# Padding a ring of split weights by 64 bytes a slot

## The reference, cut to what matters

```python
h = rmsnorm(x); u = h @ hgrn_w_in          # 2048 -> 10240
m = gated_recurrence(u) @ hgrn_w_out       # 2048 -> 2048
x = x + rmsnorm(m)
x = x + rmsnorm(conv_ffn(rmsnorm(x)))      # 2048 -> 11264, 5632 -> 2048
proj = rmsnorm(x) @ w_in_2                 # 2048 -> 7184
x = x + concat(stick_breaking, gated_delta) @ w_out_2
x = x + cross_attention(rmsnorm(x), rmsnorm(mem))
x = x + conv_ffn_2(rmsnorm(x))
return rmsnorm(x)
```

## Time and profile before

| | us |
|---|---|
| median of 3 runs | 2696.56 |
| lowest, highest | 2696.28, 2697.19 |
| the profiled execution | 2697.01 |
| its span, first to last instruction | 2695.2 |
| TensorE matmuls busy in it | 2683.5 |
| VectorE, ScalarE busy | 1971.6, 1335.3 |

### The profile page before, as it was taken

The page is one execution under the profiler, slowest core; times in us unless marked ns, Lnnn a source line. Parts: engine busy times, 40 slices in busy tenths (PEclk is TensorE's granted clock), DMA queues, the critical chain, the costliest instruction groups (busy, mean ns, idle before and its releaser), DMA issues.

```text
span 2695.2 us, 47424 instructions
## 1 busy us (share of the span) xinstructions
PE 2683.5 (100%) x17616; PEld 2291.9 (85%) x17616; DVE 1971.6 (73%) x2721; ACT 1335.3 (50%) x1679; POOL 133.9 (5%) x138
## 2 busy tenths in 40 slices
PE   9999999999999999999999999999999999999998
PEld 8888888888888888888888888878888888888887
DVE  6888888878888888644466677767678888885444
ACT  6455555455444444433465566665644444443443
POOL 0211121210000000000000000000000000000000
PEclk9999999999999999999999999999999999999999
DMA  7555555475555555655645544355455555556554
GB/s 245 180 165 172 165 168 173 161 196 170 189 187 187 187 187 187 195 187 187 218 139 181 170 145 139 134 171 186 150 190 187 187 187 187 187 188 197 185 184 150
DMA packets 136197, 481.68 MB, mean 179 GB/s; under 512 B 14880, under 2 KB 19120, under 8 KB 135680
## 3 DMA queue, kind: packets, MB, share of 16 engines
q1 hardware_dynamic: 134160, 472.06, 53.2%
q0 software_dynamic: 1376, 7.46, 0.8%
q10 hardware_dynamic: 528, 0.26, 0.0%
HBM read 477.63 MB, written 2.10 MB: 178 GB/s over the span
## 4 chain that ended last, share of the span: by engine, by line
PE 82%; DVE 8%; issue 4%; DMA 3%; ACT 2%; DVEq 1%; SPq 0%; ACTq 0%
PE acc L442 29%; PE acc L444 15%; PE acc L465 8%; PE acc L467 8%; PE acc L466 8%; PE acc L414 4%; DMA raw<-stream 3%; DVE wts L362 3%; PE acc L415 2%; ACT wts L355 2%; DVE cy L2313 2%; DVE cin L392 1%; DVE half L380 1%; PE ps L1406 1%; PE ps L740 1%
## 5 line engine op out<-in xcount | busy, mean ns | idle before, releaser
L442 PE MATMUL acc<-hs,wts 128*128 128x512 f32 x4640 | 1626.8, 394 | 0.0
L362 DVE TENSOR_TENSOR wts<-raw,wts 128x1024 fp32r<-128x1024 f32 x888 | 1061.9, 1227 | 525.0 <-ACT wts L355 524.3
L355 ACT ACTIVATE wts<-raw 128x1024 fp32r<-128x1024 f32 x888 | 913.6, 1055 | 847.0 <-PE acc L444 367.9
L444 PE MATMUL acc<-hs,wts 128*128 128x256 f32 x4640 | 1297.1, 280 | 0.0
L442 PEld LDWEIGHTS acc<-hs,wts 128*128 128x128 f32 x4640 | 871.0, 188 | 194.1 <-DVE wts L362 0.9
L444 PEld LDWEIGHTS acc<-hs,wts 128*128 128x128 f32 x4640 | 871.5, 188 | 0.5
L467 PE MATMUL acc<-wts,acts 128*128 128x512 f32 x688 | 272.8, 396 | 0.0
L465 PE MATMUL acc<-wts,acts 128*128 128x512 f32 x688 | 272.6, 396 | 0.2 <-DVE wts L362 0.2
L466 PE MATMUL acc<-wts,acts 128*128 128x512 f32 x688 | 270.4, 393 | 0.0
L369 ACT ACTIVATE half<-acc 128x512 f32<-128x512 f32 x161 | 95.3, 592 | 157.7 <-PE acc L444 138.9
L466 PEld LDWEIGHTS acc<-wts,acts 128*128 128x128 f32 x688 | 129.2, 188 | 32.2
(11 more groups left out here) (361 smaller groups left out, 2172.7 us busy)
## 6 DMA issues: line engine op xcount, KB each, us to landing
raw<-stream SPq DMA_DIRECT2D x888, 512.0 KB, 4.1
xf<-xT SPq DMA_DIRECT2D x8, 256.0 KB, 6.6
raw<-stream SPq DMA_DIRECT2D x8, 256.0 KB, 6.7
fm<-memT POOLq DMA_DIRECT2D x2, 1024.0 KB, 6.6
fw<-stream POOLq DMA_DIRECT2D x2, 1024.0 KB, 10.7
memr<-memT POOLq DMA_DIRECT2D x1, 2048.0 KB, 9.8
outT<-memr SPq DMA_DIRECT2D x7, 256.0 KB, 2.8
KQ<-masks POOLq DMA_DIRECT2D x1, 448.0 KB, 5.7
```

The source lines that it names most:

```text
L355: nc.scalar.activation(high, source, ACT.Copy).then_inc(hi_ready, 1)
L362: nc.vector.tensor_tensor(low, source, high.bitcast(F32), ALU.subtract).then_inc(lo_ready, 1)
L442: nc.tensor.matmul(acc[:, 2 * par + n, :], whi[:, b, c:c + P], src[:, kt, :], start=start, stop=False)
L444: mm = nc.tensor.matmul(acc[:, 2 * par + n, 0:T], wlo[:, b, c:c + P], src[:, kt, 0:T], start=False, stop=stop)
```

## The change

The ring gets 16 float32 (64 bytes) of padding behind each slot. `whi`, `wlo` and `both_parts` name the same parts of a slot as before.

```diff
-        wts = sb("wts", [P, SLOTS, 2, BLK], F32R)
-        whi, wlo = wts[:, :, 0], wts[:, :, 1]
+        wts = sb("wts", [P, SLOTS, 2 * BLK + 16], F32R)
+        whi, wlo = wts[:, :, 0:BLK], wts[:, :, BLK:2 * BLK]
...
         def both_parts(b):
 
-            return wts[:, b].rearrange("p s f -> p (s f)")
+            return wts[:, b, 0:2 * BLK]
```

## The result

The padded kernel takes 2704.7 us (median of 10 runs, 2703.2 to 2706.4) against 2697.4 for the kernel before (10 runs, 2695.8 to 2699.1): a ratio of 1.0027, with a 95% interval of 1.0017 to 1.0037. It is slower by 7 us, where the likeliest case of the prediction was no change; the rival "slots 1 and 3 lose their start" had 2704.4. The range held the time, because it had been drawn wide enough to take in that rival.

The account below looks back on a forecast made before the run. The prediction took TensorE's own matmul pace as the bound, its matmuls covering 2683.5 of 2695.2 us. All terms were 0, so the forecast was 2696.6 us, beside a median of 2696.56, with a range of 2694 to 2706.

Parts of the forecast that it names:

- slots 1 and 3 lose their start: Weight loads of lines 442 and 444: 3.3 ns a pair slower, 7.8 us, giving 2704.4; all slower cases together 0.24.
- Where the time is read: Whole kernel: time is TensorE's matmul pace; addresses matter only by changing it or by slowing VectorE or ScalarE until TensorE waits.
- the move of the other tiles: All tiles behind the ring move by 256 bytes, activations from 288 to 32: taken as 0, at most 11.3 us less.
- Slots as weights: 4704 pairs loading weights from slots, now at 128, 192, 256, 320: taken as 0, bounds 0 and 11.6 us more.
- the 3.3 that the prediction named as a sign of being wrong: Pace of pairs loading from slots: differing with a slot by more than 3.3 ns a pair would show the forecast wrong.
- rows 4 and 7: Timeline before the change: twelve pairs of lines 442 and 444 at 346.7 ns; 0.23 us matmuls before weights of remainder 128.
- Rows 5, 6 and 8: Timeline before: by-token pairs at 350.0 ns, wide matmuls at 233 ns, and 0.24 us for L2053 before weights of remainder 288.
- the slower case: Slots 1 and 3 or three slots slow as weights, or a jump that costs: chance 0.24; 2704.4 or 2708.2 from slots.
- Slots streamed: Wide products, lines 465 to 467, streaming two runs now 8256 bytes apart for 8192: taken as 0, bounds 9.8 us either way.
- Faster, by activations at 32: Rival: tiles moved from 288 to 32 load fast in by-token and wide products, 11.3 us less, 2685.3; faster chance 0.08.
- Lines of 16 bytes: Skill's rule for slots as weights: all starts alike, term 0; not leaned on, since rows show 350.0 against 346.7 ns.

## Why the prediction was right or wrong

**Where the time is read, right.** The time was TensorE's pace, and it changed by the address of what it reads. VectorE and ScalarE, the waits and the move of the other tiles were put at 0, and are: the splits take 1226 and 1055 ns, the waits add to 6.6 us as before, and the change with the tiles put back has the time of the change.

**Slots as weights, wrong in the likeliest case.** The prediction took 0, since 192 and 320 are multiples of 64. The term measured 10.3 us by the laps and 11.6 over the whole trace, with slots 1 and 3 slow, as the rival had it. The rival's 7.8 was a little small, for a block in slots 1 and 3 costs 0.03 to 0.04 us more and not 0.026. That is 4 to 5 ns a pair, beyond the 3.3 that the prediction named as a sign of being wrong. The step that failed is the sentence that "the moving operand's remainder (288, 160) leaves no mark in rows 4 and 7". It leaves none because 128 - 288 and 128 - 160 are both 96 by 128. Rows 5, 6 and 8 have 32, 32 and 0. The rows bore out the difference of two starts as well as the start of one, and I had read them for one alone. With the difference, the new slots give 96, 32, 96, 32, and the slower case is the forecast. The rival came out at the right time for a reason (multiples of 128) that the runs with activations 64 and 96 further refute. So that its 2704.4 is within 0.3 us of the measured 2704.7 is luck in part: its term was 3 to 4 us too small, and the by-token and wide products gave back 2 us that it had put at nothing.

**Slots streamed.** The prediction said that a jump between two runs has no visible price. In the change the wide products gave 1.0 to 1.2 us back. But 128 bytes of padding made the same matmuls 3.3 ns faster with the activations' start unchanged, so the streamed addresses do count, and the zero was a small term rather than none.

**Faster, by activations at 32.** 288 to 32 changed nothing by itself, as the forecast said. That a better place for them exists was in this rival. Of the five places tried for `acts` the best is 384, and it is worth 17 us.

**Lines of 16 bytes, and the other engines.** Blocks differ by up to 0.07 us in 2.77 between starts that are all multiples of 16. By the Trainium skill, "SBUF — State Buffer", section "Specifications (TRN2)", with lines of 16 bytes all these starts would be alike. The trace differs, and the measurement decides. With the writes of the ring cut to a sixteenth, most blocks kept the slow pace of 2.83 us. The Trainium skill, "SBUF — State Buffer", section "Who interferes with whom", says that TensorE waits for no other engine. With that the run agrees as far as it goes.

**What stays open.** For lines 442 and 444 over a ring of like slots the runs show a fast pace at a difference of 96 by 128, kept through delays, and mostly a slow one at 64, 32 and 0. What in the start of a stretch picks the pace at 32 and 0 isn't known. The fine form of the rule (0.05 us a block within 16 bytes), the effect of unlike slots, and the rule of the wide products (best at 0 of the differences tried, and also better with slots 128 or 32 bytes apart) are measured and not explained. What causes it, and whether the weight load or the stream is the one held up, was not shown.

## What to carry to other kernels

Where TensorE is the bound with float32r matmuls, read its pace from starts in the timeline for each kind of product and compare that with columns over clock. Unequal rests for equal shapes can come from addresses, and also from how a stretch began, so read several stretches and not one. Then try the relative start of the two tiles that it reads at once, in steps of 32 bytes up to 128, for each product by itself: a gap of 96 bytes in the right place was worth 0.6% here, and one of 64 bytes in the wrong place cost 0.85%. An edit that moves an early tile moves every tile behind it, so the move and the edit should be tried apart.

## What the runs showed of the hardware that was not expected

At a granted clock of 2.4 GHz a float32r matmul of 512 streamed columns, 213 ns by its columns, took from 226.7 to 233.3 ns in steady wide products of kernels that differ in tile addresses alone. In the kernel with activations 64 bytes further, blocks of lines 442 and 444 have two steady paces at the same addresses, 2.773 us (42 blocks) and 2.827 (422). Behind one weight load that came 0.09 us late the pace went from the first to the second and stayed there. In the kernel before, the same delay left nothing behind.
